# Two-layer attention and mixture-of-experts trunk: the last weight split of the attention loop placed behind the gate's evacuation, expert rows gathered ahead of the landing of the former results

## What is computed

```python
h  = rms_norm(x, norm1_g)
p  = h @ w_in                                   # [512, 2560], split among three head groups
y  = concat(retention(...) * silu(r_g),         # 4 heads, chunks of 256, a gate with silu
            moba_attention(...),                # 4 heads, block-sparse causal
            memory_attention(...))              # 4 heads, against 256 memory rows
x  = x + y @ w_out
t  = rms_norm(x, norm2_g)
# top-1 group of 4, then top-2 of 4 experts in it: each token goes to 2 of 16 experts
for e in range(16):
    out += combine[:, e] * ((silu(t @ w_gate[e]) * (t @ w_up[e])) @ w_down[e])
x  = x + out
```

## Time and profile before

| | |
|---|---|
| Three runs | 1256.53 us median (1255.36 to 1256.84) |
| Profiled execution, its own time | 1256.25 us |
| Its span, first to last instruction | 1254.6 us |
| PE busy in the span | 1144.6 us (91%) |
| DVE busy | 897.5 us (72%) |
| ACT busy | 698.4 us (56%) |
| POOL busy | 186.5 us (15%) |
| DMA, mean over the span | 221 GB/s |

### The profile page before, as it was taken

How to read it: one execution, slowest core, us unless ns; L and a number is a source line. 1 busy time by engine, 2 the same in 40 slices (tenths; PEclk the granted TensorE clock), 3 DMA queues, 4 the chain that set the end, 5 groups by cost and what they waited for, 6 DMA issues and landing times.

```text
span 1254.6 us, 18217 instructions
## 1 busy us (share of the span) xinstructions
PE 1144.6 (91%) x5538; PEld 917.3 (73%) x5538; DVE 897.5 (72%) x1288; ACT 698.4 (56%) x968; POOL 186.5 (15%) x238
## 2 busy tenths in 40 slices
PE   4999998999999999999279999989999999999991
PEld 3887676788777887777168876667877788877770
DVE  5467555637988988988194675556489888988973
ACT  6322322324888888887252223324248888888860
POOL 3005001001012212211400050010011212222211
PEclk9999799999999999999679997999999999999996
DMA  9522211206999979997943222112089997999965
GB/s 341 185 82 67 68 34 34 68 34 249 365 368 351 358 266 377 369 361 295 340 147 102 69 66 68 34 35 84 34 296 375 373 371 270 344 365 381 364 241 213
DMA packets 121892, 277.46 MB, mean 221 GB/s; under 512 B 13265, under 2 KB 13473, under 8 KB 121680
## 3 DMA queue, kind: packets, MB, share of 16 engines
q1 hardware_dynamic: 106912, 240.30, 53.1%
q0 software_dynamic: 14896, 36.19, 8.0%
HBM read 269.56 MB, written 23.07 MB: 233 GB/s over the span
## 4 chain that ended last, share of the span: by engine, by line
PE 70%; DMA 11%; DVE 9%; issue 5%; ACT 3%; POOL 1%; POOLq 0%; ACTq 0%; DVEq 0%
PE bank L1386 19%; PE bank L1388 18%; PE bank L1387 18%; DMA xg<-h_scratch,tok_now 5%; DMA pair_rows<-ysb,pair_now 5%; PE bank L1418 3%; PE bank L1490 2%; PE bank L1717 2%; PE bank L1511 1%; PE bank L1517 1%; PE bank L1485 1%; DMA hd<-pair_rows 1%; PE bank L1575 1%; DVE w_lo L390 1%; DVE x L925 1%
## 5 line engine op out<-in xcount | busy, mean ns | idle before, releaser
L386 DVE TENSOR_TENSOR w_lo<-stage,w_hi 128x1024 fp32r<-128x1024 f32 x244 | 294.0, 1220 | 16.0 <-ACT w_hi L381 14.5
L381 ACT ACTIVATE w_hi<-stage 128x1024 fp32r<-128x1024 f32 x236 | 246.4, 1059 | 48.0 <-PE bank L1388 48.0
L1386 PE MATMUL bank<-w_hi,hT_hi 128*128 128x512 f32 x384 | 157.5, 410 | 4.5 <-DVE hT_lo L939 4.5
L1388 PE MATMUL bank<-w_hi,hT_lo 128*128 128x512 f32 x384 | 152.6, 397 | 0.0
L1387 PE MATMUL bank<-w_lo,hT_hi 128*128 128x512 f32 x384 | 152.5, 397 | 0.0
L386 DVE TENSOR_TENSOR more_lo<-stage,more_hi 128x1024 fp32r<-128x1024 f32 x124 | 146.0, 1218 | 1.8 <-ACT more_hi L381 1.4
L381 ACT ACTIVATE more_hi<-stage 128x1024 fp32r<-128x1024 f32 x124 | 127.9, 1060 | 15.0 <-PE bank L1388 14.5
L349 ACT ACTIVATE w_hi<-stage 128x1024 fp32r<-128x1024 f32 x56 | 58.8, 1057 | 113.9 <-PE bank L1388 113.9
L390 DVE TENSOR_TENSOR w_lo<-stage,w_hi 128x1024 fp32r<-128x1024 f32 x56 | 67.9, 1220 | 74.9 <-ACT w_hi L349 73.9
L1386 PE MATMUL bank<-w_hi,xgT_hi 128*128 128x512 f32 x264 | 104.7, 396 | 1.2 <-DVE xgT_lo L1282 1.2
L1387 PE MATMUL bank<-w_lo,xgT_hi 128*128 128x512 f32 x264 | 104.9, 397 | 0.0
(11 more groups left out here) (239 smaller groups left out, 2009.5 us busy)
## 6 DMA issues: line engine op xcount, KB each, us to landing
stage<-in_w_exp_up SPq DMA_DIRECT2D x124, 512.0 KB, 5.8
stage<-in_w_exp_gate SPq DMA_DIRECT2D x122, 512.0 KB, 5.6
stage<-in_w_exp_down SPq DMA_DIRECT2D x122, 512.0 KB, 6.2
stage<-in_w_in SPq DMA_DIRECT2D x40, 512.0 KB, 4.2
stage<-in_w_out SPq DMA_DIRECT2D x16, 512.0 KB, 3.9
stage<-in_w_mem_kv SPq DMA_DIRECT2D x8, 512.0 KB, 7.5
h_scratch<-act POOLq DMA_DIRECT2D x8, 512.0 KB, 2.9
act<-pair_rows POOLq DMA_DIRECT2D x8, 512.0 KB, 6.2
```

Of the source, the lines that this page charges most:

```text
L381: eng.activation(x_hi[n % NX], src, ACT.Copy).then_inc(s_hi, 1)
L386: eng.tensor_tensor(x_lo[n % NX], src, x_hi[n % NX].bitcast(f32), ALU.subtract).then_inc(s_lo, 1)
L1386: pe.matmul(dst, l_hi, r_hi, start=start, stop=False)
L1388: return pe.matmul(dst, l_lo, r_hi, start=False, stop=stop)
```

## The change

In the attention part: a single silu of one value per partition (into the new tile `tint`) is issued on ACT after the loop, the gate's evacuation comes next, and the hi part of unit 27 after it. On DVE the lo part of unit 27 is taken from between `probs_out(23)` and `tile_out(3)` to the sixth round of the retention (`r == 5`).

In the experts: POOL's wait for the landing of a scatter is taken out of `scatter` and stands in `landed`, which comes behind the next turn's gather and ahead of its scatter. The initial count of free result buffers is 1 in place of 2, and the first `landed` adds the other. At the end of a layer the memory load stands ahead of the wait for the last but one scatter. Three semaphore increments (`apart`) are added; they touch no other engine.

```diff
@@ gpsimd
-                    def scatter(i, e2, pair16, col, landed=True):
+                    def landed(i, count):
+                        pool.wait_ge(s_yst[i], count)
+                        pool.sem_inc(s_yfree, 1)
+
+                    def scatter(i, e2, col):
                         pool.wait_ge(s_ye, e2 + (i + 2))
+                        apart(pool)
                         pool.tensor_copy(pair_now[:, i, :], slot_pair[:, bass.ds(col, 1)]).then_inc(s_pair, 1)
...
-                        if landed:
-                            pool.wait_ge(s_yst[i], pair16 + 16 + 16 * i)
-                            pool.sem_inc(s_yfree, 1)
-
-                    pool.wait_ge(s_yst[1], p * 128 + 16)
-                    pool.sem_inc(s_yfree, 2)
+
+                    pool.sem_inc(s_yfree, 1)
...
                             pool.wait_ge(s_xgt, e2 + (i + 1))
+                            apart(pool)
                             gather(i, pair * 2 + (i + 2))
                             pool.wait_ge(s_last, e2 + (i + 1))
                             apart(pool)
                             gather_dma(i, tok_now[:, i, :])
-                            scatter(i, e2, p * 128 + pair * 16, pair * 2 + i)
-                    scatter(0, E_N - 2, p * 128 + (8 * E_N - 16), E_N - 2)
+                            landed(1 - i, p * 128 + pair * 16 + 16)
+                            scatter(i, e2, pair * 2 + i)
+                    landed(1, p * 128 + 8 * E_N)
+                    scatter(0, E_N - 2, E_N - 2)
                     pool.wait_ge(s_xgt, E_N)
                     load_memory()
-                    scatter(1, E_N - 2, p * 128 + (8 * E_N - 16), E_N - 1, landed=False)
+                    pool.wait_ge(s_yst[0], p * 128 + 8 * E_N)
+                    scatter(1, E_N - 2, E_N - 1)
@@ scalar
-                    if j in FREED_AT:
+                    if j in FREED_AT and j < 23:
                         make_hi(sc, base, 20 + FREED_AT[j])
                     if j == 5:
                         evacuate(3)
+                sc.activation(tint[:, :], eps, ACT.Silu)
                 evacuate(4)
+                make_hi(sc, base, 20 + FREED_AT[23])
@@ vector
                 probs_out(23)
-                make_lo(dv, base, 20 + FREED_AT[23])
                 tile_out(3)
...
                         ins.then_inc(s_re, 1)
+                    if r == 5:
+                        make_lo(dv, base, 20 + FREED_AT[23])
```

More of the change, by code:

```diff
@@ L94, in build @@
         ss = sb("ss", [128, 16])
+        tint = sb("tint", [128, 1])
         rstd = sb("rstd", [128, 16])
```

## The result

The changed kernel took 1236.7 us (median of 4 runs, 1235.87 to 1238.22), the kernel before 1256.68 us beside it (4 runs, 1255.36 to 1260.54): ratio 0.9837, 95% interval 0.9814 to 0.9861. Forecast were 1242.5 us and a range down to 1239.6.

The account below looks back on a forecast made before the run. PE's three product lines fill over half the span, so only PE's idle time could be won: 7.8 us in attention plus 6.2 in the expert steps, 14.0 together. 1256.53 - 14.0 = 1242.5 us, range 1239.6 to 1248.5.

Parts of the forecast that it names:

- A, the split out of the way: End of the attention loop: PE's idle wait before the transposes goes, 3.24 us a layer, plus 0.65 from full clock.
- A, ACT's and DVE's part at 0: Attention end and retention: the moved ACT work and DVE's lo part fit into idle time, cost 0.
- A, the clock stays up afterwards: After the attention loop: without the idle stretch PE should stay at 2.4 GHz, gaining 0.65 us a layer.
- the clock falls anyway: Rival: transposes and small retention products run at 1.2 GHz, 1.5 us lost a layer, 1245.5 us; chance 0.11.
- B, all waits on gathers go: Expert steps: gathers issued about 5.8 us earlier land before PE asks, even by the worse bound; 7.19 us were lost.
- B, 1 us given back to the weight stream: Expert steps: weight loads become late next, taking 1 us of the 7.19 and leaving 6.2.
- PE's own step is 18.13 us: Expert steps: two turns of rows with no wait between them are 18.13 us apart, taken as PE's own step.
- the stream's ceiling at 372 GB/s: Rival, expert steps: weight loading limits a step to 18.5 us, 1247.2 us; chance 0.25, shared with the no-effect case.
- the burst of row traffic: Rival, expert steps: simultaneous scatter and gather delay weights; at 0.7 us a step 1261.4 us; chance 0.03.
- B without effect: Rival, expert steps: something else holds the gather, 1247.2 or 1248.7 us; chance 0.25, shared with the stream ceiling.
- a third cause: Anywhere in the kernel: something not seen, given no size; chance 0.01.

Follow-up runs that it names:

- A alone: Only the attention part of the change, silu written into an existing tile, against the kernel before: 1249.93 us, ratio 0.9937.
- without the tile: Attention and expert parts together, silu written into an existing tile so no address moves, against the kernel before: 1245.72 us, ratio 0.9889.
- B alone: Only the expert part (gathers ahead of the scatter's landing), no new tile, against the kernel before: 1253.17 us, ratio 0.9952.
- the run with the later gathers: Kernel before plus one unused tile and five more POOL semaphore increments ahead of each gather, against the kernel before: 1256.31 us, ratio 1.0000.
- tile alone: Kernel before plus one unused tile that moves later tiles 32 bytes, nothing else, against the kernel before: 1267.07 us, ratio 1.0062.
- the fastest: Changed kernel plus two more unused tiles, later tiles 96 bytes further than in the kernel before, run again: 1232.58 us, ratio 0.9802 to before.

## Why the prediction was right in its parts and wrong in the sum

- **A, the split out of the way** (3.24 + 0.65 = 3.9 a layer): right in kind, small in size. It gave 4.44 us in each layer at the place: 3.41 for the 3.24, and 1.03 for the 0.65, since the last copy ended 3.12 after the transposes began and not 3.5. No idle stretch, transposes 1.91 us at clock 1.00.
- **A, ACT's and DVE's part at 0**: right, with 0.40 us of idle time left behind the lo part and PE's lead unchanged through the later rounds.
- **A, the clock stays up afterwards**: right at the place, wrong for the layer. The rounds of retention kept 2.4 GHz, but the stretch at half clock at the end of the routing is 6.8 us long with A and 3.4 without it, which gives back about 1.6 us a layer. The rival "the clock falls anyway" had nearly that loss (1.5), but in the retention, where the clock stayed up. That A alone gave 7.9 us for 7.8 is these errors of opposite sign and an interval of 4.8 to 10.9, not a term that came out.
- **B, all waits on gathers go**: right. 13 steps of 18.14 us without the tile, 4.4 us regained in layer 1. The gather issued at 371.74, with the scatter under way, landed at 378.81, 7.1 us later: under both bounds (8.62 alone, and the scatter's landing ahead of it).
- **B, 1 us given back to the weight stream**: wrong. The steps without the tile kept 18.13 to the end of the loop; the stream followed to 382 GB/s in the changed kernel. In B alone the steps regained 4.4 + 2.6 = 7.0 of the 7.19 us.
- **PE's own step is 18.13 us**: this is the step of the working that failed. I took PE's work for unchanged because the change adds no PE instruction. The new tile of one value, which the text of the change names and its diff doesn't show, stood in no term. It moved the operands of 72 products a step by 32 bytes, 0.30 us a plain step. The 26 steps of the kernel with both parts took 7.2 us less with the tile than without it (235.77 and 235.78 to 232.17 and 232.22). With 14.0 that makes 21.2, 1235.3 us, against 1236.7 and 1235.35 measured.
- **The rivals**: the stream's ceiling at 372 GB/s, the burst of row traffic, and B without effect are all excluded by the turns of rows at 18.13 and 17.83 us. The range's low end was built from the upper ends of the two parts, so it left no room for a third cause, which the prediction gave 0.01.

## What to carry to other kernels

A line that allocates anything is part of a change: work out which tiles move, and look at the distance of matmul starts by operand, not at busy time (0.39 us each in both kernels). Where matmuls are like these (f32r, 512 columns), try operands at multiples of 128 bytes, and compare edits at equal addresses, or the comparison measures the shift: here it was worth half as much as the intended change. And where a DMA is issued by POOL, look at how long the issue takes and at what DVE runs beside it: quickening PE by under 2% in a kernel whose gathers have no slack made it slower, since four gathers' issues were held up beside DVE's unbroken row of splits (why these four isn't shown); first give the gather slack, as B does.

## What the runs showed of the hardware that I had not expected

- The pace of f32r matmuls of 512 columns hangs on where the operands start in SBUF: 227 to 230 ns at 0 modulo 128 bytes for all; 228 to 231 ns at 64 for the operands loaded as weights, but 233 for the one streamed operand that moved; 231 to 237 ns at 32 and 96.
- The issue of an indirect gather took POOL from 1.04 us (in the run with the later gathers) to 5.16 (tile alone), by what DVE ran. It usually ended 0.9 to 1.0 us behind the end of a DVE instruction with both inputs in SBUF, but missed up to three such ends in a row when DVE had no gap.
- The DMA engines moved 382 GB/s over 111 us in the changed kernel, 370 before, and 389 in a step of 17.69 us of the fastest.
